# First rows by matrix product, last expert unit peeled, a norm folded into the output projection, and one more late gate unit

## What is computed

```python
h = h + hybrid_mixer(rms_norm(h, norm1_w[layer]), ...)   # ends in mixed @ w_out
h = h + expert_choice_ffn(rms_norm(h, norm2_w[layer]), w_router[layer], ...)
...
def moe_swiglu(h, router, wg, wu, wd):
    logits = (t @ router).astype(jnp.float32)
    vals, idx = lax.top_k(logits, TOP_K)          # 2 of 8 experts for each token
    gates = jax.nn.softmax(vals, axis=-1)
    ...
    for e in range(N_EXPERTS_2):
        out = out + combine[:, e:e + 1] * swiglu(t, wg[e], wu[e], wd[e])
h = layer_norm(ALPHA * h + f, ln2_g[i], ln2_b[i])
```

## Time and profile before

| | |
|---|---|
| Time, median of 3 runs | 3258.61 us (3257.73 to 3263.88) |
| The profiled execution's own time | 3259.85 us |
| Its span, first to last instruction | 3257.9 us |
| PE busy | 2973.9 us (91%) |
| DVE busy | 1039.9 us (32%) |
| ACT busy | 546.9 us (17%) |
| POOL busy | 221.3 us (7%) |
| Mean DMA rate | 127 GB/s |

### The profile page before, as it was taken

How to read it: one execution, slowest core, us unless ns; L and a number is a source line. 1 busy time by engine, 2 the same in 40 slices (tenths; PEclk the granted TensorE clock), 3 DMA queues, 4 the chain that set the end, 5 groups by cost and what they waited for, 6 DMA issues and landing times. The chain is left out here.

```text
span 3257.9 us, 43583 instructions
## 1 busy us (share of the span) xinstructions
PE 2973.9 (91%) x18330; PEld 1832.2 (56%) x18330; DVE 1039.9 (32%) x1913; ACT 546.9 (17%) x1248; POOL 221.3 (7%) x204
## 2 busy tenths in 40 slices
PE   8998898998779979989999999999999599999895
PEld 4544787554333338867578884478775244444342
DVE  5666655653221234631300002119212211111013
ACT  3222322221111121133000000011340000000001
POOL 0001321340000000011000000000010000000000
PEclk9999899999879989999999999999999799999998
DMA  3411000116379921202012241012020615547926
GB/s 114 106 52 43 4 16 29 39 42 242 142 306 430 426 100 57 93 26 117 0 52 77 77 170 62 0 72 101 29 91 1 269 45 206 232 174 321 399 74 258
DMA packets 79954, 414.77 MB, mean 127 GB/s; under 512 B 10771, under 2 KB 16275, under 8 KB 64068
## 3 DMA queue, kind: packets, MB, share of 16 engines
q1 hardware_dynamic: 68028, 384.75, 29.9%
q10 hardware_dynamic: 8328, 15.40, 1.9%
q0 software_dynamic: 3456, 12.58, 1.0%
HBM read 383.69 MB, written 29.02 MB: 127 GB/s over the span
## 5 line engine op out<-in xcount | busy, mean ns | idle before, releaser
L3249 PE MATMUL pgu<-gu,xg 128*64 128x320 f32 (+1 forms) x2560 | 393.6, 463 | 8.0 <-POOLq L3192 5.6
L2884 PE MATMUL pp<-feat,lead 128*128 128x264 f32 x1408 | 315.9, 388 | 2.0 <-DVEq L2898 2.0
L3249 PEld LDWEIGHTS pgu<-gu,xg 128*64 128x64 f32 x2560 | 181.0, 137 | 205.8 <-issue 130.2
L2884 PEld LDWEIGHTS pp<-feat,lead 128*128 128x128 f32 x1408 | 269.1, 191 | 48.6 <-DVEq L2898 2.2
L372 PE MATMUL proj<-feat,w 128*128 128x512 f32 x576 | 255.9, 597 | 2.6 <-PEq L153 2.6
L2462 PE MATMUL ring<-feat,lead 128*128 128x264 f32 x1024 | 245.2, 401 | 3.0 <-PEq L2250 1.5
L2462 PEld LDWEIGHTS ring<-feat,lead 128*128 128x128 f32 x1024 | 201.0, 198 | 42.6 <-issue 6.8
L2462 PE MATMUL ring<-feat,w 128*128 128x264 f32 x896 | 208.3, 390 | 0.0
L3256 PE MATMUL py<-down,hm_t 128*64 128x512 f32 x880 | 200.1, 603 | 7.7 <-POOLq L3192 7.7
L2462 PEld LDWEIGHTS ring<-feat,w 128*128 128x128 f32 x896 | 169.9, 192 | 31.5 <-issue 3.1
L372 PEld LDWEIGHTS proj<-feat,w 128*128 128x128 f32 x576 | 107.4, 191 | 124.6 <-issue 124.6
(11 more groups left out here) (468 smaller groups left out, 3441.9 us busy)
## 6 DMA issues: line engine op xcount, KB each, us to landing
gu<-in_moe_gu SPq DMA_DIRECT2D x16, 3072.0 KB, 13.5
gu<-in_moe_gu SPq DMA_DIRECT2D x16, 2560.0 KB, 15.9
ring<-in_w_gate SPq DMA_DIRECT2D x16, 2048.0 KB, 13.7
ring<-in_w_up SPq DMA_DIRECT2D x16, 2048.0 KB, 15.3
ring<-in_w_down SPq DMA_DIRECT2D x16, 2048.0 KB, 17.6
w<-in_w_in SPq DMA_DIRECT2D x15, 2048.0 KB, 7.9
down<-in_moe_down SPq DMA_DIRECT2D x8, 3072.0 KB, 18.7
lead<-in_ffn_up SPq DMA_DIRECT2D x22, 1024.0 KB, 4.9
```

What stands on the lines that cost most here:

```text
L2884: last = pe.matmul(pp[:, b, a, half, 0:HALF], w[:, b, a, k * P:(k + 1) * P], core.feat[:, k, half * HALF:(half + 1) * HALF], start=k == 0, ...
L3249: last = pe.matmul(pgu[half(h), part, 0:n], xg[:, k, :], w[:, k, h, :], start=k == 0, stop=k == DK - 1)
```

## The change

The lines of the new kernel are shifted by about 60 down to the end of the first block, because `rms_to_features` is gone.

- `Z_LATE` is 3 instead of 2, and `z_of` gives the first period with units only a `zb`: units are now 0; 1 and 2; 3 and 4; and so on. Units 4, 8 and 12 are each a `zb`. Unit 13 is made in `late_z`, into the bank `pi`.
- The stage `rms_to_features` is gone. Its steps are done for each tile in the output projection, between its products (`turn_rows`, `scale_rows`, `move_rows`). The weights of the experts are now loaded from `expert_choice_route`, after the stored rows have landed.
- The router and the index row of block two are loaded in the mixing stage before.
- In routing VectorE makes a matrix of places `first` (for each token and each of the first 64 places, one or zero), and TensorE multiplies the rows on the chip by it: 32 products of 128 by 128 by 64. The result is copied to `xg` in the routing stage. The first rows are no longer loaded; rows of unit 1 are loaded first.
- The loop runs one unit fewer and the last unit is written out behind it. Its `y` isn't stored. A matrix `share` (token by place in the last unit, with the weight in it) is turned on TensorE, and `share_t` times `y` gives the last unit's part for all tokens. The gathers start when all other units are stored and the buffers that they write are free. `combine` adds gathered rows with nothing accumulated, and `combine_last` adds the product from PSUM.

```diff
@@ class GateWeights / gated_delta
-    Z_LATE = 2
+    Z_LATE = 3
-        z_from = GH + 2 - z_units // 2
+        z_from = GH + 2 - (z_units + 1) // 2
         def z_of(n):
-            return (2 * (n - z_from), 2 * (n - z_from) + 1) if n >= z_from else (None, None)
+            last = 2 * (n - z_from)
+            return last - 1 if last > 0 else None, last if last >= 0 else None
@@ ssd_and_output, tensor
+                def turn_rows(t):
+                    pe.wait_ge(row_scaled, t + 1)
+                    if t >= 2:
+                        pe.wait_ge(row_moved, 2 * (t - 1))
+                    for k in range(DK):
+                        last = pe.transpose(row_out(t, k), core.o_acc[:, t, k * P:(k + 1) * P], ident)
+                    last.then_inc(row_turned, 1)
                 for t in range(TILES):
                     pe.wait_ge(out_read, t + 1)
                     contract(1, 0, t)
                     contract(1, 1, t).then_inc(out_made, 1)
+                    if t:
+                        turn_rows(t - 1)
+                turn_rows(TILES - 1)
@@ ssd_and_output, scalar
+                for t in range(TILES):
+                    act.wait_ge(out_read, TILES + t + 1)
+                    act.activation(row_scratch, core.hid[:, t, :], ACT.Square, accum_out=rstat[:, 0, t:t + 1]).then_inc(row_squared, 1)
+                    act.wait_ge(row_meaned, t + 1)
+                    act.activation(rstat[:, 2, t:t + 1], rstat[:, 1, t:t + 1], ACT.Sqrt).then_inc(row_root, 1)
+                    act.wait_ge(row_scaled, t + 1)
+                    act.dma_start(A["choice_rows"][tl(t), :], core.o_acc[:, t, :]).then_inc(route.stored, 16)
+                    if t:
+                        move_rows(t - 1)
+                move_rows(TILES - 1)
@@ expert_choice_route
+            @block.sync
+            def _(sp):
+                sp.wait_ge(choice.stored, 16 * TILES)
+                weights.first_loads(sp)
@@ route_top_two, sync
                 weights.first_loads(sp)
-                sp.wait_ge(weights.rows_in, 32)
-                for part in range(2, PARTS):
-                    weights.load(sp, 0, part)
@@ route_top_two, tensor
+                pe.wait_ge(weights.first_found, 1)
+                for j in range(4):
+                    for h in range(2):
+                        k = h * 4 + j
+                        for t in range(TILES):
+                            last = pe.matmul(px[:, j * P + h * UT:j * P + (h + 1) * UT], core.hid[:, t, k * P:(k + 1) * P],
+                                             weights.first[:, t, :], start=t == 0, stop=t == TILES - 1)
+                last.then_inc(weights.first_turned, 1)
@@ route_top_two, scalar
-                act.wait_ge(weights.scattered, 2 * TILES * 16)
-                weights.load_rows(act, 0)
@@ route_top_two, vector
+                for a in range(2):
+                    out = hit if a else weights.first
+                    do(dve.tensor_tensor(out[:, :, :], each(row[:, 0:UT], TILES), over(placed[:, :, a], UT), ALU.is_equal))
+                dve.tensor_tensor(weights.first[:, :, :], weights.first[:, :, :], hit[:, :, :], ALU.add).then_inc(weights.first_found, 1)
...
+                dve.wait_ge(weights.first_turned, 1)
+                do(weights.features(dve, px))
@@ expert_ffn, sync
+                for part in range(2, PARTS):
+                    weights.load(sp, 0, part)
@@ expert_ffn, gpsimd
                 pool.wait_ge(all_stored, 1)
+                last = last_unit(pool)
+                for part in range(2):
+                    pool.wait_ge(part_done[part], last + 1)
+                    pool.sem_inc(got_free, 1)
+                pool.wait_ge(got_free, 2)
@@ expert_ffn, scalar
-                with act.Fori(0, total) as s:
+                with act.Fori(0, last) as s:
+                    gates(s)
...
-                act.wait_ge(rows_in, total * 32 + 64)
                 act.sem_inc(all_stored, 1)
+                gates(last, more=False)
@@ expert_ffn, tensor
+                with pe.Fori(0, last) as s:
+                    unit(s)
+                unit(last, final=True)
+                pe.wait_ge(share_out, 1)
+                pe.wait_ge(y_out, last + 2)
+                for t in range(TILES):
+                    if t >= 2:
+                        pe.wait_ge(combined, 2 * TILES + t - 1)
+                    for h in range(2):
+                        added = pe.matmul(pgu[:, t % 2 * 2 + h, :], share_t[half(h), t * P:(t + 1) * P], y[half(h), :], start=True, stop=True)
+                    added.then_inc(last_added, 1)
@@ expert_ffn, vector
+                unit(last, final=True)
+                dve.wait_ge(enlarged, TILES + 1)
+                combine(0)
+                combine(1)
+                rows_out(last)
+                combine(2)
+                combine(3)
...
-                combine(0)
+                combine_last(0)
                 for t in range(1, TILES):
-                    combine(t)
+                    combine_last(t)
                     finish(t - 1)
                 finish(TILES - 1)
```

222 lines of the change are left out of this document (122 added, 100 removed).

## The result

The changed kernel takes 3230.61 us at the median of 4 runs (3228.57 to 3239.59), beside 3259.48 for the kernel before in the same runs: ratio 0.9914, 95% interval 0.99 to 0.9929. That is 28.9 us or 0.86% faster. The forecast was 42 us, 3217, with a range of 3209 to 3230, so the sign was right, the forecast gain was 1.45 times what came, and the median lies 0.6 us above the range. The profiled execution has a span of 3229.2, 28.7 less than before. TensorE is now busy 93% of it.

A forecast was written before the change was run, and what follows sets the result against it. TensorE, busy 91% of the span, was taken as the bound, with idle stretches at four places. Terms 15.5 + 6.0 + 11.0 + 9.5 = 42.0 us off 3259.85 gave 3217.9, 3216.6 at the median; range 3209 to 3230.

The forecast's parts named there:

- Gate units: Gated delta stage: removing three waits for weights (9.7 us) and slow products behind two of them (5.8) gains 15.5 us.
- it is hidden: Gated delta stage: each 4.9 us load of gate weights fits in some 20 us between two units.
- comes back in `late_z` (3.62) and cancels: Gated delta stage: the unit leaving the first period (3.62 us) costs the same in `late_z`, so no net change.
- partly fictitious: Gated delta stage: the waits move to other engines' work, leaving half of 15.5 us, 3224 in all; chance 0.1.
- Norm: Output projection: one tile's chain instead of four behind the last addition, router product 6.3 us earlier; 6.0 us taken.
- feared collision of gathers with weights: First expert product of block one: gathers and weights share transfers for some us; 6.0 us taken, 3 as lower end.
- Routing: Block two: tables loaded earlier and first rows made by TensorE end the first expert unit 11 us earlier.
- 7.25 + 2.2 = 9.4: Routing: the 64-record first-rows product starts at the lower clock, rises, and takes 9.4 us.
- rival with chance 0.2: Routing: the first-rows product stays at the low clock, gain 6.9 us instead of 11, 3221 at the median; chance 0.2.
- work-out at full clock: Routing: with the first-rows product at full clock throughout, the gain is 13 us.
- Last unit: End of kernel: earlier gathers and four additions ahead of the last `y` copy gain 9.5 us.
- They start near 3205: Last unit: gathers wait only for the previous unit's stores (3203.7) and freed buffers; before, they started at 3226.25.

The follow-up runs named there:

- gate units alone: The kernel before with only the gate units' change (`Z_LATE` 3, new `z_of`, bank `pi`): ratio 0.9976, gate stretch 276.08 us.
- earlier first unit: The changed kernel with the first gate unit made one period earlier and two units in `late_z` instead of three: ratio 0.9894, gate stretch 268.27 us.
- all edits: Changed kernel with first gate unit earlier, unread products before router and first-rows products, down parts after unit 1's rows, gathers outside GpSimd's loop: 3223.35 us, ratio 0.9877.

## Why the prediction was too high

**What bounds the kernel** was right at all four places: each part gains in its own stretch.

**Gate units, 15.5 forecast, 5.9 measured.** The waits are gone, and the slow products behind them too; the step that failed is "it is hidden" and "comes back in `late_z` (3.62) and cancels". The load is hidden from the gate unit, but not from TensorE's own instruction fetch: without the loads the stretch is 4.65 shorter. And the moved unit didn't cancel: it had filled a wait for VectorE, so that it saved 0.4 in its periods and cost 3.45 in `late_z`, 3.0 us. The other 1.9 of the gap are open. They lie in the periods with stops: those are 7.4 us longer than the sum had them (3.2 from 439.47 on, 4.2 in the last part), of which the loads explain 4.65, and the waiting periods gave 0.9 more than summed. The idle 1.37 near 542, which is there without loads too and not in the trace before, may have a part in it. The rival "partly fictitious" gave half the term, for another reason (waits that move to VectorE and ScalarE); the price was near, the mechanism only in the unit's part.

**Norm, 6.0 forecast, 4.8 measured** (6.9 less the turns' 2.1). The path to the router product was right: 6.23 from the last addition, where the sum had 6.8. The missing term is the clock: TensorE stands 2.5 and 1.8 us beside the last tile's chain, and the router product takes 3.62 instead of 1.94, 1.7 us. The feared collision of gathers with weights didn't come: the wait for the first rows of the experts is 5.5, 5.6 before.

**Routing, 11 forecast, 7.1 measured.** The step "7.25 + 2.2 = 9.4" failed: the clock didn't rise during the product, 13.92 instead of 9.4. It was the rival with chance 0.2, at 6.9 (its own bound, 13.84 less 9.4, makes it 6.6). It should have had more: of the two bounds in the earlier trace rows, one was a run of the same kind of loads behind idle time, and it had not risen in 13.84 us; I trusted the expert product of the earlier trace rows, which is of another shape. And the work-out at full clock, 13 us, was wrong too: with the product at 7.28 the stretch is 3.7 us longer than before the change (78.42 against 74.70), as the scatters are then not hidden.

**Last unit, 9.5 forecast, 7.9 measured.** The count of 16 operations behind the copy held (22.23 against 21.8). "They start near 3205" failed, though the store behind it was right: GpSimd stood in its loop until the last down part landed, so the gathers started 7 us later than the sum had them, counted from the unit's start, and the copy was 3.0 late. Taking the last unit out of the loop gave 2.85 back: there the gathers start 16.6 behind the last `y` copy but one, where the sum had 15.8.

**What the forecast did not have.** The stretch to the last addition holds 2.1 us of added turns and yet is 0.4 shorter. Before, the first contraction of the output projection ran at the lower clock (5.40 us for 8 records), after, it did not (3.70):

```profile
736.92 3.70 PE L1428 MATMUL proj<-steps_and_weighted,chan 128*128 128x512 f32 x8 [1.42 <-ACT chan L1524]
```

It came and went between kernels with the same code at this place (5.4 in the kernel before and in nine of the twelve experiments, 3.7 in the changed kernel, with the gate units alone, with the earlier first unit and with all edits), so it goes with the timing. It is worth 1.7 us in this product, and the changed kernel's stretch is 1.9 to 2.6 shorter than in the four kernels that share its code up to there and ran the product slowly. So some 2 us of the 28.7 in this trace are luck; what decides it is open.

Sum of the misses: 9.6 + 1.2 + 3.9 + 1.6 = 16.3, less 2.5 for this stretch (2.1 + 0.4) and 0.5 at the start, is the 13.3 between 42.0 and 28.7.

## What to carry to other kernels

A transfer that is moved under an engine's work is hidden only if that work doesn't need transfers itself: look at how many instructions it runs. Here a stretch of very short ones needed a packet of 16 KB every 4 us or so, and got none until the end of a load of 1024 KB. Before work is moved from one place to another, ask in both places whether the engine would otherwise wait; here a unit inside a wait cost 0.4 us, and moved out of it 3.45. And when a slow step ends earlier, list what was still in flight beside it: here a product at half the clock kept 10 MB of weights out of the way of scatters that the next unit needed.

## What was not expected of the hardware

- A 16 KB packet of TensorE's instructions moved some 3 us later when a load of 1024 KB was in flight, at the load's end there as in 20 other loads, and TensorE stood for 1.87 and 1.65 us (1.61 and 1.58 with the gate units alone) in the middle of runs of 32 x 32 products. As four loads of 256 KB the same bytes left 0.48 near 440.
- A product of 64 records with 128 x 128 weight loads and 64 columns stayed at the lower clock for all of its 13.92 us behind a wait of 4.14, and ran in 7.28 behind unread products. The expert product of the earlier trace rows, also behind idle time, rose within its first half.
- Eight scatters of rows that land within 6.5 us of their last issue when no load is issued behind them took 20.8 us when 10.7 MB of weight parts were issued from that moment on.
